# A reordered instruction plan, and SiLU by ScalarE's own function, in a hybrid attention and feed-forward kernel

## What is computed

```
def _half_ffn(x, g, w_gate, w_up, w_down):            # w_gate, w_up (1024, 2816), w_down (2816, 1024)
    h = _rmsnorm(x, g)
    return x + 0.5 * ((jax.nn.silu(h @ w_gate) * (h @ w_up)) @ w_down)

x = _half_ffn(x, ...)                                  # first feed-forward
z = _rmsnorm(x, g_mix) @ w_in                          # 1024 -> 2500 columns: queries, keys, values, index
o_a = _diff_attention(...)                             # 4 heads, softmax(part 0) - lam * softmax(part 1), sub-RMSNorm
o_b = _dsa_attention(...)                              # 8 heads over the top k keys of a 4-head indexer
x = x + concat(o_a, o_b) @ w_out
x = _half_ffn(x, ...)                                  # second feed-forward
```

## Time and profile before

| | |
|---|---|
| median of the runs | 2892.51 us |
| the profiled execution | 2897.2 us, of which the span is 2895.3 us |
| mean granted clock of TensorE | 0.952 |
| busy: TensorE, its weight loads | 2575.2 us (89%), 2200.0 us (76%) |
| busy: VectorE, ScalarE, GpSimd | 1520.7 us (53%), 940.5 us (32%), 126.8 us (4%) |
| chain that ended last | TensorE 71%, VectorE 10%, issue 8%, ScalarE 5%, DMA 4% |

### The profile page before, as it was taken

How to read it: one execution, slowest core, us unless ns; L and a number is a source line. 1 busy time by engine, 2 the same in 40 slices (tenths; PEclk the granted TensorE clock), 3 DMA queues, 4 the chain that set the end, 5 groups by cost and what they waited for, 6 DMA issues and landing times.

```text
span 2895.3 us, 36415 instructions
## 1 busy us (share of the span) xinstructions
PE 2575.2 (89%) x13547; PEld 2200.0 (76%) x13547; DVE 1520.7 (53%) x3016; ACT 940.5 (32%) x1726; POOL 126.8 (4%) x203
## 2 busy tenths in 40 slices
PE   7999999998899968778699777878798979999997
PEld 6899999786677646666578767877798878877776
DVE  4445544543444338765445357877655534444443
ACT  3222222332222224433224335653333322222221
POOL 0000000032000000000003100000000000000000
PEclk9999999999999979998899988999899999999999
DMA  4232122334334142322333431222111122322221
GB/s 174 75 126 73 59 88 73 122 121 136 113 135 126 50 137 75 100 72 70 109 117 128 151 102 59 68 78 72 57 45 59 58 90 95 114 97 88 87 88 58
DMA packets 244076, 271.29 MB, mean 94 GB/s; under 512 B 72096, under 2 KB 196544, under 8 KB 243904
## 3 DMA queue, kind: packets, MB, share of 16 engines
q1 hardware_dynamic: 243904, 268.98, 28.4%
HBM read 235.21 MB, written 35.29 MB: 93 GB/s over the span
## 4 chain that ended last, share of the span: by engine, by line
PE 71%; DVE 10%; issue 8%; ACT 5%; DMA 4%; SPq 1%; DVEq 0%; ACTq 0%
PE bank L1136 10%; PE bank L1137 10%; PE bank L1138 10%; PE bank L1153 6%; PE bank L1154 5%; PE bank L1155 5%; PE bank L1173 4%; PE bank L1175 4%; PE bank L1174 4%; ACT w_hi L1438 3%; PE bank L1263 2%; DVE w_lo L1721 2%; PE bank L1398 1%; PE bank L1246 1%; PE bank L1193 1%
## 5 line engine op out<-in xcount | busy, mean ns | idle before, releaser
L1721 DVE TENSOR_TENSOR w_lo<-raw,w_hi 128x1024 fp32r<-128x1024 f32 x320 | 390.3, 1221 | 330.1 <-ACT w_hi L1438 329.7
L1136 PE MATMUL bank<-XTh_a,w_hi 128*128 128x320 f32 x1408 | 450.6, 320 | 3.1 <-DVE w_lo L1721 2.9
L1137 PE MATMUL bank<-XTl_a,w_hi 128*128 128x320 f32 x1408 | 442.6, 314 | 0.0
L1138 PE MATMUL bank<-XTh_a,w_lo 128*128 128x320 f32 x1408 | 442.3, 314 | 0.0
L1438 ACT ACTIVATE w_hi<-raw 128x1024 fp32r<-128x1024 f32 x320 | 332.5, 1048 | 230.4 <-PE bank L1175 181.7
L1153 PE MATMUL bank<-w_hi,hid_hi 128*128 128x512 f32 x792 | 329.8, 416 | 42.5 <-issue 23.2
L1154 PE MATMUL bank<-w_lo,hid_hi 128*128 128x512 f32 x792 | 318.5, 402 | 0.0
L1155 PE MATMUL bank<-w_hi,hid_lo 128*128 128x512 f32 x792 | 317.1, 400 | 0.0
L1136 PE MATMUL bank<-XTh_b,w_hi 128*128 128x512 f32 x704 | 295.9, 420 | 0.0
L1137 PE MATMUL bank<-XTl_b,w_hi 128*128 128x512 f32 x704 | 284.9, 405 | 0.0
L1138 PE MATMUL bank<-XTh_b,w_lo 128*128 128x512 f32 x704 | 284.5, 404 | 0.0
(11 more groups left out here) (311 smaller groups left out, 3896.7 us busy)
## 6 DMA issues: line engine op xcount, KB each, us to landing
raw<-in_w_gate SPq DMA_DIRECT2D x44, 1024.0 KB, 5.0
raw<-in_w_up SPq DMA_DIRECT2D x44, 1024.0 KB, 5.0
raw<-in_w_down SPq DMA_DIRECT2D x44, 1024.0 KB, 4.8
raw<-in_w_in SPq DMA_DIRECT2D x16, 1024.0 KB, 4.9
s_k_in<-in_cache_diff_k SPq DMA_DIRECT2D x16, 512.0 KB, 5.5
s_v_in<-in_cache_diff_v SPq DMA_DIRECT2D x8, 1024.0 KB, 5.7
raw<-in_w_out SPq DMA_DIRECT2D x8, 1024.0 KB, 4.9
kT_b<-kT_scr SPq DMA_DIRECT2D x10, 512.0 KB, 3.6
```

Source lines behind the costliest of these rows:

```text
L1136: pe.matmul(out, hi[:, k], XTh[g][:, k, lo:up], start=(k == 0), stop=False)
L1137: pe.matmul(out, hi[:, k], XTl[g][:, k, lo:up], start=False, stop=False)
L1138: last = pe.matmul(out, low[:, k], XTh[g][:, k, lo:up], start=False, stop=(k == KD - 1))
L1721: dve.tensor_tensor(hilo(w_lo, u)[:, :, 0:width_of(u)], raw_part(u), hilo(w_hi, u)[:, :, 0:width_of(u)].bitcast(F32), ALU.subtract).then_i ...
```

## The change

The feed-forward's SiLU becomes one ScalarE activation (`Silu`), which also frees the bank; the VectorE operation behind it goes, and the factor at the down product becomes 0.5. In the plan:

- `Stream.pair` begins the down matmuls one gate part later (two for group B) and spreads them evenly over the rest of the gate parts.
- `merge` puts no side item behind the last main items ahead of a `late`, and knows an item `PAUSE`, which has a weight and no instruction.
- The splits of weight units come behind a following main item, and never between a chunk's last part and its `late`.
- In the attention of a group, `q_load`, `near` and `values` are issued at the start, with pauses; `q_turn(b+1)` stands ahead of block b's scores, and `q_load(b+3)` behind it; `o_take(b-1)` stands behind `mix(b)`.
- The sample stage issues its first key loads at its start, followed by a pause; the stages begin with a pause; the second `o_load` has a weight of 6.0.

```diff
@@ Stream.pair @@
+        parts = [[(w, j, c, k) for j in range(F_PAIR) for c in range(len(CHUNKS[g])) for k in range(0, KD, K_PART[g])] for w in range(2)]
+        downs = [] if self.prev is None else [("down", self.prev, h, i) for h in range(2) for i in range(len(TILES[PAIRS[self.prev][1]]))]
+        wait = 2 if g == GB else 1
+        sent = 0
+        for n, part in enumerate(parts[0] + parts[1]):
+            w, j, c, k = part
+            self.put(("gu", p) + part)
+            if w and k + K_PART[g] == KD:
+                self.late = ("late", p, j, c)
+            upto = 0 if n < wait else min(len(downs), math.ceil(len(downs) * (n - wait + 1) / (len(parts[0]) - wait)))
+            while sent < upto:
+                self.put(downs[sent])
+                sent += 1
@@ merge @@
+    owed = {m for k, m in enumerate(main) if any(x[0] == "late" for x in main[k + 1:k + 3]) and m[0] != "late"}
...
-        while n < len(side) and cum * total * share <= spent * weight:
+        while n < len(side) and m not in owed and cum * total * share <= spent * weight:
@@ out_items @@
-    out = [(0.1, ("o_load", tag, 0)), (0.1, ("o_load", tag, 1))]
+    out = [(0.1, ("o_load", tag, 0)), (6.0, ("o_load", tag, 1))]
@@ att_items @@
-    out = [(0.1, ("near_zero", g)), (0.1, ("k_load", g, 0)), (0.1, ("k_load", g, 1)), (2.0, ("k_split", g, 0))]
+    out = [(0.1, ("near_zero", g)), (0.1, ("k_load", g, 0)), (0.1, ("k_load", g, 1))]
+    out += [(0.1, ("q_load", first)), (0.1, ("q_load", first + 1))]
+    out += [(0.1, ("near", HEADS * g + m)) for m in range(NEAR_RING)] + [(0.1, ("values", 5 * g + m)) for m in range(2)]
+    out += [(4.0, PAUSE), (2.0, ("k_split", g, 0))]
...
+    out += [(2.0, ("q_turn", first)), (0.1, ("q_load", first + 2))]
     out += [(0.1, ("keys", 10 * g + m)) for m in range(K_RING)]
-    out += [(0.1, ("values", 5 * g + m)) for m in range(2)]
-    out += [(0.1, ("near", HEADS * g + m)) for m in range(NEAR_RING)]
-    out += [(0.1, ("q_load", first)), (0.1, ("q_load", first + 1)), (0.8, ("q_turn", first))]
+    out.append((5.0, PAUSE))
...
+        if i + 1 < n:
+            out.append((0.8, ("q_turn", b + 1)))
+            if i + 3 < n:
+                out.append((0.1, ("q_load", b + 3)))
         if i < n:
             scores(b, 0)
-        if att2:
-            out.append((0.4, ("o_take", b - 2)))
...
-        if i + 1 < n:
-            out.append((0.8, ("q_turn", b + 1)))
-            if i + 2 < n:
-                out.append((0.1, ("q_load", b + 2)))
...
+        if att1:
+            out.append((0.4, ("o_take", b - 1)))
@@ sample_items @@
+    out = [(0.1, ("x_begin",))] + [(0.1, ("x_k_load", 0, h)) for h in range(2)] + [(0.1, ("x_new_load", b)) for b in range(2)]
+    out += [(8.0, PAUSE), (1.0, ("x_q", "dq")), (0.6, ("x_q", "iq")), (0.6, ("x_q", "w")), (1.0, ("x_key", "i", 0)),
@@ make_plan: both merges of attention begin with PAUSE, of 5.0 (group A) and 4.0 (group B) @@
@@ Plan.__init__ @@
+            if waiting and (item[0] == "late" or age and item[0] in ("gu", "down", "mm") and raw[n + 1][0] != "late"):
+                for k in waiting:
+                    split(k)
+                waiting = []
+            if after.get(n):
+                waiting += [k for _, k in after[n]]
+                age = 0
+            elif item[0] in ("gu", "down", "mm"):
+                age += 1
@@ ScalarE, gu @@
-                        act.activation(part, out_of(key)[:, 0:up - lo], ACT.Tanh, scale=0.5).then_inc(tanh_ready, 1)
+                        act.activation(part, out_of(key)[:, 0:up - lo], ACT.Silu).then_inc(frees(key), 1)
@@ VectorE, gu and down @@
-                    if w == 0:
-                        dve.wait_ge(tanh_ready, plan.tanh_no[key] + 1)
-                        dve.scalar_tensor_tensor(part, part, 1.0, out_of(key)[:, 0:up - lo], ALU.add, ALU.mult).then_inc(frees(key), 1)
-                    else:
+                    if w:
...
-                    dve.scalar_tensor_tensor(x, out_of(key)[:], 0.25, x, ALU.mult, ALU.add).then_inc(frees(key), 1)
+                    dve.scalar_tensor_tensor(x, out_of(key)[:], 0.5, x, ALU.mult, ALU.add).then_inc(frees(key), 1)
```

More of the change, by code:

```diff
@@ L310, in merge @@
     return out
+PAUSE = ("pause",)
 def norm_items(tag, n):
@@ L425, in sample_items @@
 def sample_items():
-    out = [(0.1, ("x_begin",)), (1.0, ("x_q", "dq")), (0.6, ("x_q", "iq")), (0.6, ("x_q", "w")), (1.0, ("x_key", "i", 0)),
+    out = [(0.1, ("x_begin",))] + [(0.1, ("x_k_load", 0, h)) for h in range(2)] + [(0.1, ("x_new_load", b)) for b in range(2)]
+    out += [(8.0, PAUSE), (1.0, ("x_q", "dq")), (0.6, ("x_q", "iq")), (0.6, ("x_q", "w")), (1.0, ("x_key", "i", 0)),
            (0.1, ("x_key_load", "i", 2)), (1.2, ("x_q", "sq"))]
@@ L435, in sample_items @@
             out.append((1.2, ("x_combine", p - 1)))
-    out += [(0.1, ("x_k_load", 0, h)) for h in range(2)] + [(0.1, ("x_new_load", b)) for b in range(2)]
     out += [(1.2, ("x_combine", BATCH_PAIRS - 1))]
@@ L516, in make_plan @@
     s.flush()
-    plan += merge(s.take(), [(0.1, ("enter", GA))] + sample_items() + [(0.1, ("fence",))] + att_items(GA) + [(0.1, ("reload", GA))]
+    plan += merge(s.take(), [(5.0, PAUSE), (0.1, ("enter", GA))] + sample_items() + [(0.1, ("fence",))] + att_items(GA) + [(0.1, ("reload", GA))]
                   + out_items("ota", 5), share=0.98)
@@ L525, in make_plan @@
         s.pair(pair_no(1, GA, f))
-    plan += merge(s.take(), [(0.1, ("enter", GB))] + att_items(GB) + [(0.1, ("reload", GB))] + out_items("otb", 4), share=0.98)
+    plan += merge(s.take(), [(4.0, PAUSE), (0.1, ("enter", GB))] + att_items(GB) + [(0.1, ("reload", GB))] + out_items("otb", 4), share=0.98)
     s.proj("O", GB)
@@ L577, in __init__ @@
         first_main = next(n for n, i in enumerate(raw) if i[0] == "gu")
+        waiting, age = [], 0
         for n, item in enumerate(raw):
@@ L582, in __init__ @@
             self.items.append(item)
-            for _, k in after.get(n, ()):
-                split(k)
+            if waiting and (item[0] == "late" or age and item[0] in ("gu", "down", "mm") and raw[n + 1][0] != "late"):
[7 more added lines that the diff above has]
+                age += 1
+        assert not waiting
         self.number()
@@ L900, in build @@
         unit_done = sem("unit_done")
-        tanh_ready = sem("tanh_ready")
         hid_hi_ready = sem("hid_hi_ready")
```

## The result

The changed kernel takes 2784.6 us (median of 4 runs, 2782.06 to 2787.89) against 2890.9 us (a fourth execution of the kernel before took 2888.37 us), a ratio of 0.963 with a 95% interval of 0.961 to 0.965: 106 us faster. The forecast was 2760 us. Its profiled execution took 2782.9 us, with a mean granted clock of 0.966 after 0.952.

What follows compares the result with a forecast made beforehand. Hand-offs in fixed queues were taken to bound the merges. Terms 52 + 40 + 43 + 28 + 47 = 210 us gained, less 75 us for table loads, gave 135 us, so 2760 us; range 2670 to 2900.

Steps and rivals of the forecast that it cites:

- the likeliest case: Whole kernel: the forecast itself, 2760 us, counted as met between 2700 and 2830 us; chance 0.43.
- The plan: All reordering of queues, with the clock: 210 us gained, before 75 us given back for table loads.
- What is late next: After `o_take` moves: `mix`, then score banks, would be late, and VectorE gains a wait; half of 86.7 us taken, 43.
- The borders: Loads first, with pauses, at stage borders: 52 of 95.4 us of TensorE waits go; bounds 15 and 95.
- Queries ahead: Query turn before the preceding block's scores: 40 of 41.9 us of score matmul waits go; lower bound 20.
- `o_take`: Attention, right after `mix`: 43 of 86.7 us of TensorE's waits for output banks go; bounds −20 and 87.
- Downs: Feed-forward down matmuls, later splits and side work: 28 of 23.2 + 16.3 us of waits go; bounds 16 and 39.
- Clock: Merges and the projection between: fewer waits mean less time at the low clock, 47 us gained; bounds 10 and 75.
- Silu: ScalarE gate activation: 98 table loads, 126 us, 75 of it on the path; VectorE's 73.2 us less work worth 0.
- rival 1: ScalarE: Silu shares Exp's table, so 210 us are gained, about 2680 us; chance 0.13.
- Rival 2: Merges: waits come back elsewhere, leaving 18 us gained, near 2875 us, or 2830 to 2885 with part; chance 0.26.
- Rival 3: ScalarE queue in merges: table loads delay exponentials, 3.4 us each; slower, 2957 us with 80 loads; chance 0.18, in-between outcomes included.

Runs made afterwards that it cites:

- the last experiment: Changed kernel with a block's weigh matmuls and `o_take` moved behind the first score of the next block but one: 2758.4 us, ratio 0.954 to the kernel before.

## Why the prediction was right, point by point

The direction, the range and the likeliest case held: the time is 25 us above the forecast. But two of its parts were wrong in opposite directions, and that they nearly cancel is luck: the plan gives 98 us less than its 210, and Silu takes 5 us of them back, which can't be told from nothing, in place of 75. Of the signs named beforehand, these came: no wait for the query before the score matmul, no waits of 1.63 us before the downs of the last stage, that stage 19 us shorter, and 96 loads. The two merges became 40 and 48 us shorter, in place of 50 and 60.

- *The plan.* I summed 210 us; the plan alone gives 112. The failed step is "What is late next" under `o_take`, and my general discount: I let 163 of the touched 263.5 us go. In fact 197 went, and 105 us of new waits came up. I had named some (score banks, `mix`) but not priced them. The largest, `pT` with 64 us in place of 13, I had named as a sign without a price, and put down to the loads after the result; without them it is still 53 to 61 us, so the plan makes most of it.
- *The borders.* 52 us plus clock expected; alone they gave 35, and in the changed kernel the waits there fell from 95 to 59 us, by 36. That the keys would be late in the place of the queries was right: 14.4 us.
- *Queries ahead.* I priced it at 40 us by itself. Measured, it costs 45 us alone and gains 28 in its place. My lower bound of 20 was wrong, for I looked at the lag of `q_lo` and not at the banks.
- *`o_take`.* I took 43 of 86.7 us; in its place it is worth 69 (107 − 38), alone 31. The queue on VectorE that I gave as the reason isn't the whole of it, as the last experiment shows: at the same place, with the weigh matmuls right ahead of it, the bank waits are 16.3 us. What the added VectorE wait costs was not separated from this.
- *Downs.* 28 us expected. The last stage's 16 us of waits went as worked out, with 19 us of span; the 5 us of the first stage too. Alone it gave 18, as it lengthened a merge.
- *Clock.* 47 us expected, 21.6 us of busy time measured. New waits are followed by low stretches like the old: behind the 5.79 us wait for `pT_a` that ends at 1105.91 us the granted clock is 0.50 for 4.3 us, with TensorE busy throughout.
- *Silu.* 98 loads forecast from changes of place, 96 found (100 on the old plan), so rival 1 fell. 75 us on the path were expected; it was 36, on both plans. The relief of VectorE, which I put at 0, was 5 us on the old plan and 31 on the new. The net is a loss of 31 us on the old plan and of 5 us on the new, which can't be told from nothing.
- The Trainium skill's 2.66 us for each switch (ScalarE: Activation LUTs, "What ACT_TABLE_LOAD costs") is not borne out as a sum of ScalarE's time. The load takes 1.283 us as the page has it, but the activation behind it starts 0.01 to 0.02 us after the load wherever nothing else is late, and the median over the 96 loads is 0.02 us. Nor is there such a time before them: the 40 loads ahead of the exponentials at line 1572 have 0.7 us of idle time before them in all.
- Rival 2 (waits come back) is what happened to half of the plan's gain. Rival 3 named a real mechanism, a load that reaches TensorE at up to 3.4 us each; at 36 us for 96 it is 0.4 us each on average.

That loads before exponentials are cheap where they run in the wait for VectorE is read from the trace (30 of 46). A kernel that separates the two kinds of load was not run, so how the 36 us divide between them stays open.

## What to carry to other kernels

Edits to a fixed order aren't additive: the four plan parts alone sum to −31 + 45 − 18 − 35 = −39 us, together they give −112. Put the operation that frees a bank of a ring close behind the one that fills it, with few others in between that ask for a bank, and judge a part by taking it out of the whole as well as by adding it alone. When a wait goes, list what each queue still owes at that point; about half of the time removed here came back, and half of that as waits for copies that stand behind other work of ScalarE. A function that costs table loads can nearly pay for itself where the engine that it relieves has become what others wait for (31 against 36 us), and not where it has not (5 against 36 us).

## What the runs showed of the hardware

- Silu and Exp don't share a table here: each change between them is one ACT_TABLE_LOAD of 1.283 us. Copy and Square run behind either without a load, and so does Sign: there are 96 loads, and none of them stands before a Sign, Square (but the first instruction) or Copy.
- A table load for an activation that waits on a VectorE result ran ahead of that wait (30 of 46 are followed by over 0.1 us of waiting), while those before the gate's Silu came after the wait for TensorE's bank: 15 of the 48 had it ahead of them, 36.7 us in all, and 47 are followed by the activation within 0.1 us. So in this kernel the one kind is often hidden by a late operand and the other isn't.
- Work on an engine that is 66% busy can count: with Tanh on the new plan VectorE works for 475 of the 718 us of the second merge, and taking 132 operations of 0.55 us away shortens the kernel by 31 us. Of that, 17 us are idle time of TensorE in the profiled executions and the rest busy time, at a mean granted clock of 0.973 after 0.966. On the old plan the same 73 us of work were worth 5.
